# First attention with f32 weighing and q's halves stacked in partitions: a two-layer transformer kernel on one Trainium2 core

## What is computed

```python
def block_attention(q, k, v):
    ...
        s = jnp.einsum('bqhgd,bkhd->bhgqk', qi, k, preferred_element_type=jnp.float32) * scale
        p = jax.nn.softmax(s, axis=-1).astype(v.dtype)
        return jnp.einsum('bhgqk,bkhe->bqhge', p, v)
...
    q = rms_norm(q.reshape(b, n, GQA_HEADS, GQA_HEAD_DIM), q_norm)
    k = rms_norm(k.reshape(b, n, GQA_KV_HEADS, GQA_HEAD_DIM), k_norm)
    if rotate:
        q = apply_grid_rope(q, rope)
        k = apply_grid_rope(k, rope)
...
    y_lat = block_attention(q_lat, k_all, v_all) @ w_o
    y_ctx = block_attention(q_ctx, k_ctx, v_ctx) @ w_o
```

## Time and profile before

| | us |
|---|---|
| median of 3 runs | 2874.82 (2874.57 to 2875.98) |
| the profiled execution, its own time | 2874.26 |
| its span, first to last instruction | 2872.5 |
| PE busy | 2607.8 (91%) |
| DVE busy | 1445.7 (50%) |
| ACT busy | 1041.1 (36%) |
| POOL busy | 743.6 (26%) |

### The profile page before, as it was taken

How to read it: one execution, slowest core, us unless ns; L and a number is a source line. 1 busy time by engine, 2 the same in 40 slices (tenths; PEclk the granted TensorE clock), 3 DMA queues, 4 the chain that set the end, 5 groups by cost and what they waited for, 6 DMA issues and landing times.

```text
span 2872.5 us, 39059 instructions
## 1 busy us (share of the span) xinstructions
PE 2607.8 (91%) x16373; PEld 1442.9 (50%) x16584; DVE 1445.7 (50%) x2179; ACT 1041.1 (36%) x1713; POOL 743.6 (26%) x985
## 2 busy tenths in 40 slices
PE   4789999889999998889999999887898998899997
PEld 1346665645556576357654445544543333344443
DVE  2336884773342125688664422665765653433322
ACT  2335773333231113567543322322342213422221
POOL 1220000248787722400040000033253543011100
PEclk7899999999999999999999999999989999999998
DMA  6220003345552221210035532221112323233321
GB/s 222 103 88 16 2 2 118 115 160 189 197 176 84 93 75 49 67 59 2 30 118 186 189 109 90 78 96 52 52 52 73 99 70 110 59 103 103 99 96 55
DMA packets 206078, 268.26 MB, mean 93 GB/s; under 512 B 8975, under 2 KB 188558, under 8 KB 196686
## 3 DMA queue, kind: packets, MB, share of 16 engines
q1 hardware_dynamic: 199758, 243.97, 26.5%
q0 software_dynamic: 5280, 18.64, 1.8%
q10 hardware_dynamic: 864, 3.15, 0.3%
HBM read 252.62 MB, written 10.49 MB: 92 GB/s over the span
## 4 chain that ended last, share of the span: by engine, by line
PE 69%; DVE 16%; ACT 5%; issue 3%; POOL 3%; DMA 3%; SPq 0%; POOLq 0%; DVEq 0%; ACTq 0%
PE PS L289 19%; PE PS L288 19%; PE PS L290 19%; DVE WB L284 2%; PE PS L487 2%; PE PS L851 2%; DVE SM L933 2%; DVE AR L939 2%; ACT WB L274 1%; DMA WS<-in_mlp_w 1%; DMA WS<-in_gqa_w_qkv 1%; DVE X L1216 1%; DVE GT L1225 1%; PE PS L632 1%; PE PS L1999 1%
## 5 line engine op out<-in xcount | busy, mean ns | idle before, releaser
L289 PE MATMUL PS<-H,WB 128*128 128x512 bf16 (+1 forms) x1953 | 686.2, 351 | 30.5 <-DVE WB L284 10.5
L288 PE MATMUL PS<-H,WB 128*128 128x512 bf16 (+2 forms) x1907 | 668.2, 350 | 25.5 <-DVE WB L284 13.7
L290 PE MATMUL PS<-H,WB 128*128 128x512 bf16 (+2 forms) x1949 | 683.5, 351 | 1.2
L284 DVE TENSOR_TENSOR WB<-WS,WB 128x2048 bf16<-128x2048 f32 (+3 forms) x165 | 375.5, 2276 | 583.4 <-ACT WB L274 583.3
L274 ACT ACTIVATE WB<-WS 128x2048 bf16<-128x2048 f32 (+3 forms) x165 | 295.5, 1792 | 663.5 <-PE PS L290 424.9
L288 PE MATMUL PS<-AR,WB 128*128 128x512 bf16 (+1 forms) x1279 | 431.6, 337 | 15.8 <-DVE WB L284 7.6
L289 PE MATMUL PS<-AR,WB 128*128 128x512 bf16 (+1 forms) x1280 | 431.7, 337 | 8.1 <-DVE AR L1615 4.8
L290 PE MATMUL PS<-AR,WB 128*128 128x512 bf16 (+1 forms) x1281 | 431.7, 337 | 1.1
L288 PEld LDWEIGHTS PS<-H,WB 128*128 128x128 bf16 x1976 | 194.4, 98 | 298.5 <-issue 65.2
L290 PEld LDWEIGHTS PS<-H,WB 128*128 128x128 bf16 x1976 | 195.2, 99 | 176.4 <-issue 9.2
L289 PEld LDWEIGHTS PS<-H,WB 128*128 128x128 bf16 x1976 | 194.9, 99 | 165.5 <-issue 7.7
(11 more groups left out here) (399 smaller groups left out, 3781.3 us busy)
## 6 DMA issues: line engine op xcount, KB each, us to landing
WS<-in_mlp_w SPq DMA_DIRECT2D x64, 1024.0 KB, 5.6
WS<-in_w_ada SPq DMA_DIRECT2D x48, 1024.0 KB, 5.0
WS<-in_w_in SPq DMA_DIRECT2D x26, 1024.0 KB, 5.1
WS<-in_ada_w SPq DMA_DIRECT2D x24, 1024.0 KB, 4.9
WS<-in_ffn_w_in SPq DMA_DIRECT2D x44, 512.0 KB, 4.8
e_scratch<-EB POOLq DMA_DIRECT2D x16, 512.0 KB, 3.7
EB<-e_scratch POOLq DMA_DIRECT2D x16, 512.0 KB, 3.6
WS<-in_ffn_w_out SPq DMA_DIRECT2D x8, 1024.0 KB, 5.4
```

Source lines behind the costliest of these rows:

```text
L284: e.tensor_tensor(lo, staged(i), hi, SUB).then_inc(dv.sem, dv.mark(("lo", i)))
L288: e.matmul(out_, l[0], r[0], start=start, stop=False)
L289: e.matmul(out_, l[0], r[1], start=False, stop=False)
L290: return e.matmul(out_, l[1], r[0], start=False, stop=stop)
```

## The change

The projections: q's high and low halves are made in the buffer of the unit, and four DMAs, issued by ACT in `first` of unit u+4, bring them to `q_`, where the two halves of one head now lie above each other: one in partitions 0 to 63, the other in 64 to 127. k already lies in both. v is kept once, in f32, with a 65th column of ones for each key head; DVE has no part in it.

The first attention (`stacked`): scores are two products with 128 rows instead of three with 64. The turned exponentials are copied from PSUM once, in f32: of a latent unit the first part by ACT, the second by DVE; of a context unit the whole by ACT. Weighing is one f32 matmul for 128 keys, with 65 columns; the last column is the sum of the exponentials, and the reciprocal is taken from it. ACT's exponential has no row sum. In both attentions the output turn, its two halves and nothing else move from step u+5 to u+6.

```diff
-        V_ = arena2(12288, 6, 256)
+        V_ = arena(12288, 6, 260).rearrange("p a (h n) -> p a h n", n=65)
...
         def qkv_act(e):
+            def move(u):
+                key, s = QU[u]
+                po.wait_ge(e, ("q low", u))
+                q = at_q[u % 6]
+                hi, lo = q_halves(u)
+                e.dma_start(q_at(2 * key, LO, s), hi[LO]).then_inc(q.sem, q.mark())
+                e.dma_start(q_at(2 * key, HI, s), lo[LO]).then_inc(q.sem, q.mark())
+                e.dma_start(q_at(2 * key + 1, HI, s), hi[HI]).then_inc(q.sem, q.mark())
+                e.dma_start(q_at(2 * key + 1, LO, s), lo[HI]).then_inc(q.sem, q.mark(("q", u)))
+
             def first(u):
                 key, s = QU[u]
                 raw, sq, n = qkv_bufs(u)
                 high_halves(e, next_tiles("qkv", key // 2))
+                if u > 3 and QU[u - 4][0] < 8:
+                    move(u - 4)
                 pe.wait_ge(e, ("qkv", key, s))
-                if u > 5:
+                if u > 5 and QU[u - 6][0] < 8:
+                    at_q[u % 6].wait_ge(e, ("q", u - 6))
+                elif u > 5:
                     dv.wait_ge(e, ("turned", u - 6))
                 e.activation(sq, ps(bank_of["qkv", key, s], n), SQUARE).then_inc(ac.sem, ac.mark(("sq", u)))
...
-            def v(j):
-                ac.wait_ge(e, ("v0", j))
-                e.tensor_tensor(V_[:, 1, j, :], ps(bank_of["v", j], 256), V_[:, 0, j, :], SUB).then_inc(dv.sem, dv.mark(("vv", j), ("free", ("v", j))))
...
         def qkv_pool(e):
+            e.memset(V_[:, :, :, 64:65], 1.0).then_inc(po.sem, po.mark("v ones"))
...
+                    if A.stacked:
+                        e.matmul(o, q, x[0], start=True, stop=False)
+                        m = e.matmul(o, q, x[1], start=False, stop=True)
+                    else:
+                        m = mm3(e, o, q, x, True, True)
...
+                if A.stacked:
+                    for i, (a_, b_) in enumerate(A.parts):
+                        Q.whole(u, i)[1].wait_ge(e, ("whole", t, u, i))
+                        for k in range(a_, b_):
+                            m = e.matmul(o, Q.PT[u % 3][:, k, :], A.v(e, k, h), start=k == 0, stop=k == A.nk - 1)
...
-                if whole := Q.group_at(i - 5):
+                if whole := Q.group_at(i - 6):
                     out_turn(*whole)
...
+            def take(u):
+                if u > 2:
+                    pe.wait_ge(e, ("W", t, u - 3))
+                pe.wait_ge(e, ("T", t, u, 0))
+                e.activation(Q.whole(u, 0)[0], Q.turned_at(u, 0), COPY).then_inc(ac.sem, ac.mark(("whole", t, u, 0), ("free", ("T", t, u, 0))))
...
+            def take(u):
+                if u > 2:
+                    pe.wait_ge(e, ("W", t, u - 3))
+                pe.wait_ge(e, ("T", t, u, 1))
+                e.tensor_copy(Q.whole(u, 1)[0], Q.turned_at(u, 1)).then_inc(dv.sem, dv.mark(("whole", t, u, 1), ("free", ("T", t, u, 1))))
```

More of the change, by code:

```diff
@@ L621, in k_at, with q_at, q_halves @@
             return k_[r, 0, i, o0:o0 + n], k_[r, 1, i, o0:o0 + n]
-        def q_at(m, s):
+        def q_at(head, r, s):
             o0, n = SEG[s]
-            return q_[:, 0, m, o0:o0 + n], q_[:, 1, m, o0:o0 + n]
+            return q_[r, head % 2, head // 2, o0:o0 + n]
+        def q_halves(u):
+            raw, sq, n = qkv_bufs(u)
+            return sq.bitcast(BF)[:, 0:n], sq.bitcast(BF)[:, n:2 * n]
         def qkv_pe(e):
@@ L803, in __init__ @@
                 self.n = len(order)
-                self.steps = self.n + 6
+                self.steps = self.n + 7
             def scores_at(self, u):
@@ L814, in pt, with whole @@
                 return [self.PT[u % 3][:, j, a_:b_, :] for j in range(2)]
+            def whole(self, u, i):
+                a_, b_ = self.order[u][0].parts[i]
+                return self.PT[u % 3][:, a_:b_, :], (ac, dv)[i]
             def turned_at(self, u, i):
@@ L888, in exponent @@
                     pe.wait_ge(e, ("T", t, u - 3, Q.last_part(u - 3)))
+                dv.wait_ge(e, ("max", t, u))
+                if A.stacked:
+                    e.activation(Q.p(u), Q.scores_at(u), EXP, bias=Q.largest(u)).then_inc(ac.sem, ac.mark(("exp", t, u), ("free", ("S", t, u))))
+                    return
                 if r > 7:
                     dv.wait_ge(e, ("out", A.tag, r // 4 - 2))
-                dv.wait_ge(e, ("max", t, u))
                 e.activation(Q.p(u), Q.scores_at(u), EXP, bias=Q.largest(u), accum_out=A.sums(r)).then_inc(ac.sem, ac.mark(("exp", t, u), ("free", ("S", t, u))))
             def high(u):
+                if Q.order[u][0].stacked:
+                    take(u)
+                    return
                 for i in range(len(Q.order[u][0].parts)):
@@ L921, in divide @@
                 ac.wait_ge(e, ("exp", t, u))
-                e.reciprocal(sums, sums).then_inc(dv.sem, dv.mark())
-                pe.wait_ge(e, ("O", A.tag, g))
+                if A.stacked:
+                    pe.wait_ge(e, ("O", A.tag, g))
+                    e.reciprocal(sums, A.O_at(g)[:, :, 64]).then_inc(dv.sem, dv.mark())
+                else:
+                    e.reciprocal(sums, sums).then_inc(dv.sem, dv.mark())
+                    pe.wait_ge(e, ("O", A.tag, g))
                 if g > 1:
@@ L926, in divide @@
                 dv.wait_ge(e)
-                e.tensor_tensor(A.OT[g % 2].rearrange("p (h n) -> p h n", n=64), at(("O", A.tag, g), 256).rearrange("p (h n) -> p h n", n=64), sums.unsqueeze(2).to_broadcast([128, 4, 64]), MUL).then_inc(dv.sem, dv.mark(("out", A.tag, g), ("free", ("O", A.tag, g))))
+                e.tensor_tensor(A.OT[g % 2].rearrange("p (h n) -> p h n", n=64), A.O_at(g)[:, :, 0:64], sums.unsqueeze(2).to_broadcast([128, 4, 64]), MUL).then_inc(dv.sem, dv.mark(("out", A.tag, g), ("free", ("O", A.tag, g))))
             def largest(u):
@@ L935, in low @@
             def low(u):
+                if Q.order[u][0].stacked:
+                    if len(Q.order[u][0].parts) > 1:
+                        take(u)
+                    return
                 for i in range(len(Q.order[u][0].parts)):
```

52 lines of the change are left out of this document (28 added, 24 removed).

## The result

The changed kernel takes 2886.6 us (median of 6 runs, 2881.7 to 2889.3), the kernel before on the same chip 2874.9 (2873.9 to 2876.7). The ratio is 1.0042, with a 95% interval of 1.003 to 1.0054. So it is slower, by 11.7 us, where 15.6 were forecast. The profiled execution has a span of 2884.2 us and a time of its own of 2886.1.

What follows compares the result with a forecast made beforehand. The prediction took TensorE (PE), busy 172.35 of 180 us in the steady first attention, as the bound. Its terms +3.5 - 4 + 0.7 + 14.4 + 3 - 2 = +15.6 us on 2874.26 gave 2890 us, range 2867 to 2906.

Steps and rivals of the forecast that it cites:

- the case I had called likeliest: Whole kernel: the main forecast of 2890 us, slower by 15.6 us, chance 0.54.
- steady attention, 8 periods: First attention: twelve units take 26.0 us against 25.6, +0.4 us eight times, +3.5 us.
- start of the attention: First attention's start: fewer DVE subtractions, shorter waits and some clock given back; -4 us, bounds 0 and -9.
- its end: First attention's drain: two weighings 0.75 and 0.2 us longer, with less switching; +0.7 us.
- issues on the chain: Projections: four DMA issues at 0.45 us ahead of eight even SQUAREs; +14.4 us, bounds 11 and 22.
- lost clock in the projections: Projections: lower clock after longer PE idles, 1.2 us lost in each of three pairs; +3 us, bounds 0 and 5.
- Part 1: First attention, PE's columns and loads: f32 passes at 0.111 us, twelve units in 24.6 us against 25.6.
- rival 3: First attention's weighing: loads don't overlap, each f32 pass takes 0.165 us; +48 us, 2938 us, chance 0.03.
- Part 2: First attention's output turns, one step later: waits of about 0.55 us, together 1.4 us in twelve units.
- Rival 2: First attention: waits at output turns hide because ACT and DVE are light; 2867 us, chance 0.12.
- Part 3, the price and the place: Projections: ACT's q DMA issues, 0.45 us each, lie ahead of eight even SQUAREs; +14.4 us, lost clock +3.
- Part 4: Second attention: with output turns a step later, DVE has caught up after its divide; -2 us, bounds +1 and -5.

Runs made afterwards that it cites:

- e8: The changed kernel with v 77 columns wide instead of 65: 2887.4 us.
- e2: The changed kernel with the output turns back one step earlier (u+5) in both attentions: 2880.4 us.
- e6: The kernel before with the q part alone, its DMA moves issued by ACT behind the SQUARE: 2850.9 us.
- e4: The kernel before with the q part alone, its DMA moves issued by ACT ahead of the SQUARE: 2870.6 us.
- e5: The changed kernel with the q moves issued behind the SQUARE in even units only, ahead of it in odd ones: 2866.8 us.
- e1: The changed kernel with all q moves issued behind the SQUARE, not ahead of it: 2866.7 us.
- e11: The changed kernel with the q moves issued by POOL after its subtraction, none by ACT: 2866.7 us.
- e3: The changed kernel without its q part (64-row halves, three score products, no moves), so the weighing part alone: 3119.8 us.
- e7: The changed kernel with the first attention's scores reading only the first 64 of 128 rows of q and k: 3087.5 us.

## Why the prediction came out as it did

The forecast of 2890 is 3.4 us above the median, and the case I had called likeliest is the one that happened. That the total came so near is in part luck: the terms miss by 1 to 5 us each, some up and some down. By its steps, from two profiles of each kernel:

| term | forecast | measured |
|---|---|---|
| steady attention, 8 periods | +3.5 | +4.2 |
| start of the attention | -4 | -9.3 |
| its end | +0.7 | +1.8 |
| issues on the chain (PE's added idle time in the projections) | +14.4 | +12.3 |
| lost clock in the projections | +3 | +6.3 |
| second attention | -2 | 0 |
| everything else | 0 | -4 (-1 to -7, mostly scatter) |

**Part 1 held, to a hundredth.** 0.111 us a pass, no late starts, and the forecast lengths in a latent unit's rows, 0.65 us of scores and 1.29 of weighing. e8 bears out the reason given, the load. The rule of Part 3 in the Trainium skill's page "TensorE: Matmul & The Clock Gate" (loads overlap only in other row groups), my rival 3, is contradicted: these loads and passes use the same 128 rows and together take 0.111 us, not 0.165.

**Part 2, the waits, held.** 0.55 us where 0.55 was read off the banks, two of them in a period, and 26.13 us where 26.0 was said. Rival 2 (they hide) is out. e2 shows the price of the later place, 6.2 us; one of the two waits stays at the earlier place too.

**The start was mis-sized**, -9.3 for -4, just beyond its bound of -9. The first v sums to the first weighing take 24.7 instead of 28.2 us (-3.4), and the first twelve units 24.65 instead of 30.0 (-5.4, or -5.9 against their steady growth). The kernel before, that stretch:

```profile
232.70:271.40 38.70, 34.52 (x320) 23.49 (x321) 26.23 (x46) 23.41 (x55) 0.00 (x0) 0.82 0.09 28
```

Its clock is 0.82 there, the changed kernel's 1.00 from 254.80 to 284.30. 0.18 of 38.7 is at most 7 us of work at full clock; I had seen the 0.75 of the earlier trace rows and put it down as "some clock". Why the clock holds is open: of the two kernels with the q part alone, e6 is at 1.00 in its first twelve units (25.07 us), e4 at 0.89 (26.73 us), both with DVE's subtractions in place.

**Part 3, the price and the place.** Place: right, and e5 shows it to the unit, eight even SQUAREs. Price: an issue takes not 0.45 but 0.61 to 0.63 us (the first of four 0.47, mostly beneath EXP), and yet the waits grew by 12.3 us, less than the 14.4 forecast. The two errors go opposite ways: four issues are 2.06 us on the chain shown above, but in every second of the eight ACT has a weight tile to split, and there the issues run beneath that 1.9 us instruction. The eight even SQUAREs are late by 2.05 us four times and by 0.26 to 0.78 us four times, 10.4 us in all; the other 1.9 us of PE's idle time I can't place. The term that was off is the **lost clock**. PE's part of the projections, the kernel before:

```profile
60.50:213.20 152.70, 122.65 (x595) 58.44 (x604) 62.99 (x95) 57.13 (x101) 43.09 (x33) 0.89 0.28 96
```

PE is busy 122.65 us here and 129.76 in the changed kernel with the same products (124.2 and 129.7 in the second profiles; each trace lacks some records, 595 are kept of this one and 605 of the second). That is +7.1 and +5.5, on average +6.3 us of slower passes where I had counted three pairs, +3. What is left of the stretches, PE's idle time, grew by 13.3 and 11.4 us, the 12.3 of the table. I had taken one idle of 2.6 us and guessed how many of eight longer idles would end in the lower clock. e1, e5 and e11 give both back at once (-20 us), so the runs don't separate them; the split is by busy and idle time of two traces.

**Part 4 fell.** The second attention is unchanged at 9.39 us for four units with the turns at either step, and so is the wait. In the 100 us of the earlier trace rows the changed kernel has

```profile
PE PS L911 <- DVE AR L1001: 3.4, 10, 0.3
```

which is the row of before to the digit. I had said that by the later step DVE would have caught up. But L1001 is not the divide; it is the subtraction that frees a bank of the ring "T". By the program the output turn comes behind both parts of a unit just turned, which hold both banks, at either step; so it waits 0.34 us for the first of them, with DVE busy 89.57 of 100 us. That reading is from the program and this row, and no run separates the ring from DVE's load.

**Where the forecast could have been more useful.** It gave one sum for the whole. The runs show parts that add up as long as the stacked q is there: it is worth -24 us if its moves stay off the chain; their place costs 20; the f32 weighing costs 9 to 14 on top of it and its output turns another 6. But the weighing alone, without the q part, costs 245 us, a case that no row of before pointed to.

## What to carry to other kernels

Ask of every DMA that an engine issues what stands behind it in that engine's program: four issues of 0.6 us ahead of one SQUARE cost 20 us in eight places, and nothing that shows behind that SQUARE or on an idle engine. Before you move work from one engine to another, ask how long each of them stands waiting: here the f32 passes gave PE 6.9 us more work in twelve units, of which 4.8 fell into time in which it had stood anyway. Price short f32 passes by what their weight loads last, not by their columns. Put each idle that you add to a chain of dependent steps down twice: once as time, and once as lower clock in what follows, which here was about half as much again (6.3 us for 12.3).

## What the runs showed of the hardware

- TensorE can stay at 1.2 GHz while the profile draws it as busy nearly without a gap: for 457 us in e3 (239 to 696 us) and 409 us in e7, after a wait of 1.62 and 1.43 us, with scores of 64 rows beside f32 passes of 65 columns. The same columns with 128 rows, after the same wait of 1.43 us, ran at 2.4 GHz. One of six executions of e3 lost less (2994 us).
- A DMA issue from SBUF to SBUF takes 0.61 to 0.63 us of ACT's queue (0.47 the first of four), 0.52 to 0.56 us of POOL's. Issues on ACT run beneath an ACTIVATE that is still under way.
- f32 passes with new weights each follow each other at 0.111 us with 65 as with 77 columns (12 passes in 1.29 and 1.30 us).
